# A gated short convolution with tokens on partitions, its token shift made by DMAs of ScalarE's queue

## The reference, cut to what matters

```python
proj = rms_norm(x, pre_mix_g) @ w_in          # u, gate_b, gate_c: 1024 channels each; c_q, c_kv, k_rope
y_conv = gate_b * short_conv_causal(gate_c * u, conv_w)     # depthwise, 3 taps, causal in the tokens
y_conv = group_rms_norm(y_conv, conv_out_g, 8)              # 8 groups of 128 channels
... # 8 heads of attention with low-rank q and kv -> y_attn, 1024 channels
y = concatenate([y_conv, y_attn]) @ w_o
x = x + rms_norm(y, post_mix_g)
x = x + rms_norm(square(relu(rms_norm(x, pre_mlp_g) @ w_up)) @ w_down, post_mlp_g)
```

## Time and profile before

| | us |
|---|---|
| median of 3 runs | 1068.28 (1066.87 to 1068.4) |
| profiled execution | 1067.39 |
| its span, first to last instruction | 1065.6 |
| TensorE busy | 1053.6 |
| VectorE busy | 695.2 |
| ScalarE busy | 515.9 |
| GpSimd busy | 80.7 |

### The profile page before, as it was taken

How to read it: one execution, slowest core, us unless ns; L and a number is a source line. 1 busy time by engine, 2 the same in 40 slices (tenths; PEclk the granted TensorE clock), 3 DMA queues, 4 the chain that set the end, 5 groups by cost and what they waited for, 6 DMA issues and landing times.

```text
span 1065.6 us, 13494 instructions
## 1 busy us (share of the span) xinstructions
PE 1053.6 (99%) x4794; PEld 877.0 (82%) x4794; DVE 695.2 (65%) x785; ACT 515.9 (48%) x666; POOL 80.7 (8%) x94
## 2 busy tenths in 40 slices
PE   9999999999999999999999999999999999999996
PEld 7898888888888788888888888888888888888885
DVE  6475566679975876575575665756657656565666
ACT  7575545565544664444444444444444444444443
POOL 0011022110000310000000000000000000000003
PEclk9999999999999999999999999999999999999998
DMA  9786667864586465776666756666576665676562
GB/s 345 261 300 218 201 184 272 271 221 151 204 307 198 125 212 157 237 226 197 209 184 212 231 172 232 196 199 212 170 236 216 203 211 159 220 232 190 181 242 79
DMA packets 125619, 225.78 MB, mean 212 GB/s; under 512 B 8464, under 2 KB 30096, under 8 KB 124816
## 3 DMA queue, kind: packets, MB, share of 16 engines
q1 hardware_dynamic: 125152, 224.89, 64.7%
q10 hardware_dynamic: 432, 0.44, 0.1%
HBM read 210.08 MB, written 7.34 MB: 204 GB/s over the span
## 4 chain that ended last, share of the span: by engine, by line
PE 85%; issue 11%; DVE 2%; POOL 1%; DMA 1%; ACT 0%; SPq 0%; DVEq 0%; POOLq 0%; ACTq 0%
PE ps L725 28%; PE ps L727 28%; PE ps L726 28%; DMA raw<-in_w_in 1%; PE ps L748 1%; POOL acc L1666 0%; DVE w_lo L1305 0%; PE ps L909 0%; PE ps L914 0%; POOL x_res L1777 0%; POOL x_res L1751 0%; ACT w_hi L1005 0%; SPq L656 0%; DVE conv_s L1532 0%; DVEq L311 0%
## 5 line engine op out<-in xcount | busy, mean ns | idle before, releaser
L1305 DVE TENSOR_TENSOR w_lo<-raw,w_hi 128x1024 fp32r<-128x1024 f32 (+2 forms) x382 | 465.2, 1226 | 318.9 <-ACT w_hi L1005 316.8
L1005 ACT ACTIVATE w_hi<-raw 128x1024 fp32r<-128x1024 f32 (+2 forms) x382 | 395.8, 1038 | 460.7 <-PE ps L727 456.3
L725 PE MATMUL ps<-w_hi,xT_hi 128*128 128x512 f32 (+1 forms) x792 | 308.5, 390 | 0.6 <-DVE xT_lo L1406 0.5
L727 PE MATMUL ps<-w_lo,xT_hi 128*128 128x512 f32 (+1 forms) x792 | 305.9, 386 | 0.0
L726 PE MATMUL ps<-w_hi,xT_lo 128*128 128x512 f32 (+1 forms) x792 | 305.8, 386 | 0.0
L725 PE MATMUL ps<-w_hi,yT_hi 128*128 128x512 f32 x672 | 263.1, 391 | 0.0
L727 PE MATMUL ps<-w_lo,yT_hi 128*128 128x512 f32 x672 | 261.6, 389 | 0.0
L726 PE MATMUL ps<-w_hi,yT_lo 128*128 128x512 f32 x672 | 261.4, 389 | 0.0
L725 PEld LDWEIGHTS ps<-w_hi,xT_hi 128*128 128x128 f32 x792 | 148.7, 188 | 31.9 <-issue 2.0
L727 PEld LDWEIGHTS ps<-w_lo,xT_hi 128*128 128x128 f32 x792 | 148.6, 188 | 30.0
L726 PEld LDWEIGHTS ps<-w_hi,xT_lo 128*128 128x128 f32 x792 | 148.8, 188 | 28.7
(11 more groups left out here) (155 smaller groups left out, 425.3 us busy)
## 6 DMA issues: line engine op xcount, KB each, us to landing
raw<-in_w_up SPq DMA_DIRECT2D x64, 1024.0 KB, 5.5
raw<-in_w_down SPq DMA_DIRECT2D x64, 1024.0 KB, 5.3
raw<-in_w_in SPq DMA_DIRECT2D x28, 1024.0 KB, 6.0
raw<-in_w_o SPq DMA_DIRECT2D x16, 1024.0 KB, 5.0
aT_raw<-a_blk SPq DMA_DIRECT2D x240, 32.0 KB, 1.9
raw<-in_w_uq SPq DMA_DIRECT2D x8, 576.0 KB, 4.9
mix_rows<-blk SPq DMA_DIRECT2D x32, 128.0 KB, 2.4
raw<-in_w_ukv SPq DMA_DIRECT2D x4, 1024.0 KB, 5.3
```

What stands on the lines that cost most here:

```text
L725: nc.tensor.matmul(dst, x_hi, hi, start=first, stop=False)
L727: mm = nc.tensor.matmul(dst, x_hi, lo, start=False, stop=last)
L1005: nc.scalar.activation(w_hi[:, slot, 0:size], raw[:, raw_slot, first:first + size], ACT.Copy).then_inc(hi_ready, 1)
L1305: nc.vector.tensor_tensor(w_lo[:, slot, 0:size], raw[:, raw_slot, first:first + size], f32(w_hi[:, slot, 0:size]), ALU.subtract).then_inc( ...
```

## The change

The convolution is computed with tokens on partitions, half by half (1024 elements a partition: two token blocks by 512 channels). ScalarE's queue loads the three tap rows, broadcast to all partitions, stores the product c*u to a DRAM tensor `conv_rows`, behind two rows of zeros that SyncE stored at the start, and loads it again from one and from two rows earlier, into tiles laid over `lat` and over the rope tables. VectorE does six whole-tile operations (`conv_mix` 0 to 5: three tap products, two sums, the product with b), ScalarE the square, VectorE the sum over each group of 128 channels, GpSimd the power -1/2, VectorE the scaling; the result is turned as a batch and split by ScalarE and VectorE with the gains. TensorE's steps of the convolution are gone. The first half's split stands at chunk 105 and the second's at 115; the first half's product of the first two output strips now comes after both strips' attention quads. A root of two columns, for its table, stands behind the first half's square. The residual's rows are loaded four quads later than the gain row, and SyncE waits for the second sum of squares before the gain row. GpSimd fills two partitions of `blk` with zeros before it fills `ones`; the first turned batch waits until SyncE has stored these zeros.

```diff
--- before.py
+++ after.py
@@ -134,8 +134,6 @@
             steps.append(("lat_split", 1, 0))
         if sub == 6:
             steps.append(("krT", 0, 0))
-        if sub in (38, 54):
-            turn("conv", sub // 54)
         for p in range(PAIRS):
             at = sub - 8 - 16 * p
             if at == 0:
...
@@ -156,14 +154,20 @@
                                   (25, "o_norm", 0), (36, "o_split", 0)]:
                 if at == when:
                     steps.append((what, p, h))
-        for c in range(4):
-            for half, t, norm in [(0, 70 + 6 * c, 8), (1, 98 + 4 * c, 5)]:
-                if sub == t:
-                    steps.append(("convT", half, c))
-                if sub == t + 2:
-                    steps.append(("conv_square", half, c))
-                if sub == t + norm:
-                    steps.append(("conv_norm", half, c))
+        for h in range(2):
+            for when, what in [(4, "taps"), (34, "u_store"), (40, "u_back1"), (67, "u_back2")] if h == 0 else [
+                    (79, "taps"), (83, "u_store"), (88, "u_back1"), (88, "u_back2")]:
+                if sub == when:
+                    steps.append((what, h, 0))
+            for op, when in enumerate([(50, 56, 58, 76, 77, 83), (87, 91, 92, 94, 95, 98)][h]):
+                if sub == when:
+                    steps.append(("conv_mix", h, op))
+            for when, what in [[(84, "conv_square"), (86, "conv_stats"), (89, "conv_scale"), (105, "conv_split")],
+                               [(99, "conv_square"), (101, "conv_stats"), (104, "conv_scale"), (115, "conv_split")]][h]:
+                if sub == when:
+                    steps.append((what, h, 0))
+            if sub == (89, 104)[h]:
+                turn("conv", h)
     sub = 0
     for i, part in enumerate(CONV_PARTS):
...
@@ -179,7 +183,7 @@
         steps.append(("conv_out", i, n))
-    order = [(0, 2), (0, 3), (0, 0), (1, 2), (1, 3), (1, 0), (0, 1), (1, 1)]
+    order = [(s, q) for qs in ((2, 3), (0,), (1,)) for s in (0, 1) for q in qs]
     order += [(s, q) for s in (2, 3) for q in (2, 3, 0, 1)]
     for s, q in order:
         n = quad("out", strip=S_OUT + s, q=q, nk=4, width=W, col=s * W, first=q == 2, last=q == 1)
...
@@ -509,6 +515,7 @@
             k = m - Q_RANK // P
             return yT_hi[:, KV_AT + k], yT_lo[:, KV_AT + k], G_KV + k
+        conv_rows = nc.dram_tensor("conv_rows", (2, 2 + SEQ, W), F32, kind="Internal").ap()
         mix_rows = nc.dram_tensor("mix_rows", (4, BLK, 4, 8 * BLK), F32, kind="Internal").ap()
         def landed(batch):
...
@@ -578,15 +585,11 @@
         def token_blocks(tile, half):
             return tile[:, half * P:(half + 1) * P].rearrange("p (g i) -> p g i", g=4)
-        def conv_blocks(e, c):
-            return conv_landed(e)[:, :, :, c].rearrange("p g b i -> p b g i")
+        shifted = [lat.rearrange("p b n -> p (b n)")[:, 8 * P:16 * P].rearrange("p (b n) -> p b n", b=TB),
+                   rope[:].rearrange("p (b n) -> p b n", b=TB)]
         def by_block(tile):
             return tile.rearrange("p (b g i) -> p b g i", b=TB, g=4)
-        def conv_bank(half, c):
-            return 7 if half == 0 else 4 + c
         def wait_kv_buffers(eng, p):
...
@@ -669,15 +672,22 @@
                     load_x(n - 5)
                 if n == 7:
                     sp.dma_start(ident[:], t["ident"]).then_inc(ident_landed, 16)
-                    sp.dma_start(cos_t[:], t["cos"]).then_inc(tables_landed, 16)
-                    sp.dma_start(sin_t[:], t["sin"]).then_inc(tables_landed, 16)
+                    sp.dma_start(cos_t, t["cos"]).then_inc(tables_landed, 16)
+                    sp.dma_start(sin_t, t["sin"]).then_inc(tables_landed, 16)
+                if n == 9:
+                    sp.wait_ge(zeros_ready, 1)
+                    sp.dma_start(conv_rows[:, 0:2].rearrange("h r n -> r h n"),
+                                 blk[0:2].rearrange("p q b c i -> p (q b c i)").rearrange("p (h n) -> p h n", h=2)
+                                 ).then_inc(zeros_stored, 16)
                 for m, (_, _, after) in enumerate(batches):
                     if after == n:
                         move_batch(m)
                 if n == RESIDUAL_QUAD:
                     sp.wait_ge(oT_lo_ready, PAIRS)
+                    sp.wait_ge(ss_c_ready, 2)
                     sp.dma_start(g_post_mix[:], t["post_mix_g"].to_broadcast([P, D])).then_inc(g_mix_landed, 16)
+                if n == RESIDUAL_QUAD + 4:
                     sp.dma_start(x_res[:], x_dram).then_inc(x_res_landed, 16)
             with sp.Fori(LOOP.start, LOOP.stop) as j:
                 for i in range(8):
...
@@ -791,7 +801,7 @@
                     if z["strip"] == S_OUT and k == 0:
                         if z["q"] < 2:
-                            pe.wait_ge(convT_ready, 4 * z["q"] + 4)
+                            pe.wait_ge(convT_ready, z["q"] + 1)
                         else:
                             pe.wait_ge(oT_lo_ready, 2 * z["q"] - 2)
                     first, last = z["first"] and k == 0, z["last"] and k == 3
...
@@ -932,30 +942,6 @@
                         nc.tensor.matmul(o[1], probsT[:, h, P:2 * P], v[0], start=True, stop=False)
                         mm = nc.tensor.matmul(o[1], probsT[:, h, 2 * P:3 * P], v[1], start=False, stop=True)
                     mm.then_inc(pv_done, 1)
-                elif what == "convT" and a == 1:
...
-                elif what == "conv_norm":
...
                 elif what == "hT":
                     if a < X2_DVE:
                         pe.wait_ge(x2_ready, a + 1)
...
@@ -1171,34 +1157,47 @@
                     dst = u_sb if CONV_PARTS[a] == "u" else b_sb
                     scaled_out([dst[:, a // 3, tb] for tb in range(TB)], 2 * ((S_CONV + a) % 2), W,
                                rstd_x).then_inc(strip_out_act, 1)
-                elif what == "convT":
...
+                elif what == "taps":
                     if a:
...
+                        act.wait_ge(conv_mixed, 4)
+                    for k in range(3):
+                        act.dma_start(conv_w[:, k], t["conv_w"][0, k:k + 1, a * W:(a + 1) * W].to_broadcast([P, W])
+                                      ).then_inc(conv_w_landed, 16)
+                elif what == "u_store":
+                    act.wait_ge(strip_out_dve, a + 1)
+                    act.dma_start(conv_rows[a, 2:2 + SEQ].rearrange("(b p) n -> p b n", p=P), u_sb[:, a]
+                                  ).then_inc(u_stored, 16)
+                elif what in ("u_back1", "u_back2"):
+                    back = int(what[-1])
+                    act.wait_ge(u_stored, 16 * (a + 1))
+                    act.wait_ge(zeros_stored, 16)
+                    if a:
+                        act.wait_ge(ss_c_ready, a)
+                    elif back == 1:
+                        act.wait_ge(latT_lo_ready, 3)
+                        act.wait_ge(krT_filled, 1)
                     else:
...
+                        act.wait_ge(q_rope_ready, 4 * PAIRS)
+                        act.wait_ge(qrT_filled, PAIRS)
+                    act.dma_start(shifted[back - 1], conv_rows[a, 2 - back:2 - back + SEQ].rearrange(
+                        "(b p) n -> p b n", p=P)).then_inc(u_shifted[back - 1], 16)
                 elif what == "conv_square":
...
-                elif what == "conv_norm":
...
+                    act.wait_ge(conv_mixed, 6 * a + 6)
+                    nc.scalar.activation(shifted[0], u_sb[:, a], ACT.Square).then_inc(conv_sq_ready, 1)
+                    if a == 0:
+                        nc.scalar.activation(std_m[:], ones[:, 0:TB], ACT.Sqrt)
+                elif what == "conv_split":
+                    act.wait_ge(blk_landed, landed(("conv", a)))
+                    for c in range(4):
+                        k = 4 * a + c
+                        ins = nc.scalar.activation(by_block(yT_hi[:, k]),
+                                                   conv_landed(a)[:, :, :, c].rearrange("p g b i -> p b g i"),
+                                                   ACT.Copy, scale=gains[:, G_CONV + k:G_CONV + k + 1])
+                    ins.then_inc(convT_hi_ready, 1)
                 elif what == "y_out":
                     act.wait_ge(half_used, 2 * b + 2)
                     if a:
...
@@ -1421,12 +1422,8 @@
                     dve.wait_ge(o_normed, a + 1)
                     turn_batch(b, [o_sb.rearrange("p h b (q i) -> p (h b) q i", q=4)])
                 elif what == "conv_turn":
-                    if a == 0:
-                        dve.wait_ge(strip_out_dve, 1)
-                    else:
-                        dve.wait_ge(strip_out_act, 5)
-                    src = (u_sb, b_sb)[a]
-                    turn_batch(b, [src[:, 0, tb].rearrange("p (c q i) -> p c q i", c=4, q=4) for tb in range(TB)])
+                    dve.wait_ge(conv_scaled, a + 1)
```

(73 more changed lines are left out.)

67 lines of the change are left out of this document (13 added, 54 removed).

## The result

| | before | after |
|---|---|---|
| median, us | 1068.02 (1066.87 to 1068.40, 11 runs) | 1070.44 (1068.92 to 1071.08, 11 runs) |
| profiled execution / its span | 1067.39 / 1065.6 | 1069.78 / 1068.0 |

The ratio is 1.0021, with the interval 1.0012 to 1.003. The time lies outside the stated range (1062.0 to 1067.4) and on the other side of no change.

A forecast was written before the change was run, and what follows sets the result against it. TensorE, busy for 99% of the span in a gapless row of matmuls, was taken as the bound. 1067.39 - 5.3 removed + 1.9 stall = 1064.0, plus 0.4 for the median: 1064.4 us, range 1062.0 to 1067.4.

The forecast's parts named there:

- The removed work: On TensorE, eight sums of squares and four transposing steps of the second half go: 5.3 us saved.
- the backlog of VectorE: VectorE's bunched work makes weight splits late for TensorE between 268 and 288 us: 1.9 us of stall, 0 to 4.
- GpSimd's part: GpSimd's work that VectorE waits for: 1.41 us before `o_norm`; no wait listed between the convolution's sums and scalings.
- chunk 102: First stall: its split ends on VectorE at 270.8 us, TensorE reaches it at 270.3, 0.5 us late.
- the prediction's formula: TensorE's chunk s of weights (six matmuls) starts, less what is removed, at 237.6 + 1.364 (s - 78) us.
- (b): Landmark of the result, not a forecast: last weight matmul ahead of the last pair's `probs` transposes, at 231.27 us before.
- The root in front of the split: On ScalarE behind the first half's square: table load 1.28 us and root 0.2 us delay chunk 92's split to 252.3.
- the third rival: A drain at the root: ScalarE idle 1.4 us between load and root, everything behind later, 1065.8 us; chance 0.08.
- The rival that ends slower: Half 1's shifted rows land late through DRAM and VectorE's second mix waits: 1067.4 or 1073.9 us; chances 0.12 and 0.08.
- 8 to 12 us each before use: The first half's stores and loads through DRAM have this much time before use, so they count as hidden.
- The start: GpSimd's zero fill ahead of `ones` (0.9 us) delays TensorE's warm-up; effect on time 0 us, at most 0.5.
- What was hidden: Second half reaches TensorE with 2.8 us spare; residual's rows land at 317, used at 350.8; gain row's wait already past.

The follow-up runs named there:

- act_root: Changed kernel with the reciprocal root of the eight sums taken by ScalarE (root) and VectorE (reciprocal) in place of GpSimd; 1066.44 us, 0.9986 of before.
- all4: Changed kernel with zero fill last, rows shifted by two at chunk 72, table at chunk 80, root on ScalarE and reciprocal on VectorE; 1063.85 us, 0.9965.
- z_last: Changed kernel with GpSimd's zero fill put behind the fill of `ones`; 1070.01 us, 1.0019 of before.

## Why the prediction was wrong

- **The removed work** was right within 0.3 us: 5.3 were forecast. In the stretch where it lay it is 5.6. The version without late splits is 5.1 and 5.4 us below its before in two studies, with 0.4 to 0.5 us still lost ahead of that stretch.
- **The step that failed is the backlog of VectorE**, forecast at 1.9 us (range 0 to 4), measured at 4.5 of waiting and 5.6 with what follows the waits. In "its list is: five splits, sum, two mixes of half 1, scale, turns" no wait stands between the sum and the scaling, and none in the second half either. GpSimd's part, for which the prediction has 1.41 us before `o_norm`, is at nothing there, without a reason given. It works on eight columns, beside operations of VectorE, and takes 3.6 us, so VectorE idles 1.53 us before each scaling, 3.1 in all. Taking it away brought 2.5 us of waiting back. The first late split is therefore not that of chunk 102 but that of chunk 96, right behind the first of these waits; then come 102, as forecast, and 112 (chunks counted from the prediction's formula, with the lateness taken off). TensorE starts chunk 112 at 291.8 us. Less the 2.4 us by which it was late already at (b) that is 289.4, against 284.0 without stalls: 5.4 us late where the prediction had 1.7.
- **What makes up the 5.4:** 1.7 forecast, 3.1 for GpSimd, and 0.7 by which the chain began too late (the split for chunk 92 starts at 256.54 - 2.4 = 254.1, forecast 253.4). This 0.7 fits the split at 244.05, which took 2.02 us in place of 1.22 while GpSimd squared the attention's output from 243.95; no run takes it away alone, so that is argued and not shown.
- **Why GpSimd's part is long.** The view by forms already showed the power at 0.72 us for two columns and 1.02 for four, 0.15 us a column; eight come to 1.6, which is what was measured next to an idle VectorE. The other 0.85 us, of 2.49, are blocking. The Trainium skill, "SBUF — State Buffer", section "Who interferes with whom", makes the port pair that the two engines share an exclusive lock; the 2.48 and 2.49 us with a split running at the start, against 1.64 without one, agree.
- **The root in front of the split** was priced right: moving it took 1.5 us off the waits, the load took 1.28 us, and no drain is seen in front of it or behind (the load starts 0.02 us after the square's end, the root 0.02 us after the load's). So the third rival falls.
- **The rival that ends slower had the right kind of place and the wrong victim.** The shifted rows were never late: those of the second half, on which the rival rests, landed 4.1 and 5.4 us after issue, at 263.1 and 264.9, and the mixes that take them start at 266.28 and 271.87. But the load of the first half's rows and the last pair's batch of keys and queries were issued within 1 us, on two queues:

```profile
218.30 0.37 ACTq L1185 DMA_DIRECT2D rope<-conv_rows  x1
...
219.24 0.34 SPq L650 DMA_DIRECT2D kqT<-mix_rows  x1
```

From issue to landing, of that batch in the changed kernel, and of all twelve loads of this kind before:

```profile
DMA to landing us min/median/max: 5.9/5.9/5.9
...
DMA to landing us min/median/max: 3.1/3.3/3.4
```

TensorE waited 1.1 us, 1.3 with what follows, a term that the prediction had at nothing ("8 to 12 us each before use" asked only who waits for the new transfers, not whom they delay). Moved away from it, the wait went.
- **The clock** was no term at all. It falls in most executions of the change behind the wait of 2.2 us, for 1.6 us more. Behind shorter waits (1.74 us at 264 us in the change, 1.15 in `act_root`, 1.1 in `all4`) no profile shows a fall, so a backlog of the forecast size would probably not have brought it.
- **The start** was forecast at 0 to 0.5 us. The fill costs nothing that shows; the 0.9 us of one execution are a load that landed later.
- **What was hidden** otherwise stayed so: second half's batch, residual rows, gain row.

The terms together: 5.6 for the late splits and 1.5 for the batches (1.3, and 0.2 at the earlier one), against 5.6 removed, give +1.5 us, and +3.1 in the executions in which the clock falls. The medians, over both kinds, are 2.4 and 2.2 above.

## What to carry to other kernels

When an engine already works without rest beside a bound TensorE, its load is not the number to compare: here VectorE got less work (busy for 685.7 us, 695.2 before) and was late, since each wait in its queue (a table load before a split, a neighbour's power) comes on top of the work and uses up the slack. List the idle stretches of the new order and put other work into them; here that, and taking GpSimd out of the chain, turned +0.2% into -0.5%. For each new transfer ask which transfer with a near deadline is issued in the same microseconds.

## What was not expected of the hardware

- The granted clock can fall to half after 2.2 us without a matmul in the middle of a busy stretch, and not in every execution: it fell in five profiled executions of six with that wait (shown here is `z_last`; the one of the change is the sixth), and cost 1.6 us.
- GpSimd's small operation on eight columns takes 1.1 to 1.3 us beside a two-operand operation of VectorE and ends 0.06 us behind it; on four columns, without one, it takes 0.19 us.
- A 512 KB load lands in 3.3 us beside the weight stream alone and in 5.9 us with another of 512 KB issued 0.9 us earlier on the other queue. By the Trainium skill, "DMA: Bandwidth & Descriptors", section "Issuing engines are not separate DMA queues", both run on the same 16 engines; the trace agrees.
